# Eight places for the first weight tiles, modulation rows on GpSimd's queue, one conv group on TensorE, and block 1's top-k over two phases

## What is computed

```
mod = silu(c) @ w_ada + b_ada            # 1024 -> 6 x 1024: sh1 sc1 gt1 sh2 sc2 gt2
h1  = rmsnorm(x, g1) * (1 + sc1) + sh1
proj = h1 @ w_in + b_in                  # 512 pool, 512 conv value, 512 conv gate columns
pool_out = (box means of 2, 4, 8, 16 rows - hp) @ w_pool * pool_scale
conv_out = silu(layernorm(causal depthwise conv, 31 taps, of cv * sigmoid(cg)))
x  = x + gt1 * (concat(pool_out, conv_out) @ w_out + b_out)
h2 = rmsnorm(x, g2) * (1 + sc2) + sh2
q  = h2 @ w_query                        # 8 heads x 2 halves x 128
s  = q . sub_keys                        # 128 scores a half
top 16 of each half, top 16 of their 256 sums, softmax -> gate; 16384 experts
act = gelu(u_table[eid] . h2) * gate     # 128 rows of 4 KB for each token
x  = x + gt2 * sum(act * v_table[eid]);  y = rmsnorm(x, g_final)
```

## Time and profile before

| | |
|---|---|
| median of 3 runs | 3471.78 us (3471.12 to 3472.04) |
| profiled execution, time | 3469.63 us |
| profiled execution, span | 3467.7 us |
| mean granted TensorE clock | 0.82 |
| DMA | 1253.56 MB, mean 361 GB/s |
| VectorE, GpSimd, TensorE busy | 2125.2, 2283.7, 2206.3 us |

### The profile page before, as it was taken

One profiled execution on the slowest core, in us unless ns is written; L12 is line 12 of the kernel. 1 busy time (PEld: TensorE's weight loads), 2 busy tenths in 40 slices (PEclk: granted clock), 3 DMA queues, 4 the chain that ended last, 5 costly groups with the idle time before them and its releaser, 6 DMA issues.

```text
span 3467.7 us, 30586 instructions
## 1 busy us (share of the span) xinstructions
PE 2206.3 (64%) x9781; PEld 976.0 (28%) x9781; DVE 2125.2 (61%) x4835; ACT 360.6 (10%) x778; POOL 2283.7 (66%) x2213
## 2 busy tenths in 40 slices
PE   7873895467847899656448777454445444454576
PEld 6563452135512355211114444111111111111111
DVE  2345888645686677675655666667766776776301
ACT  3101141000111022100000010000000000000000
POOL 0012545676777777777757777777777777777675
PEclk9996897689978999888768999767777777776799
DMA  7666756899999999999989999999999999999998
GB/s 238 187 234 212 274 194 242 324 403 405 407 385 403 407 398 406 361 402 398 370 289 404 407 408 408 390 409 406 402 393 406 401 406 394 403 407 374 382 392 330
DMA packets 377968, 1253.56 MB, mean 361 GB/s; under 512 B 38056, under 2 KB 46912, under 8 KB 377793
## 3 DMA queue, kind: packets, MB, share of 16 engines
q0 software_dynamic: 304128, 1107.43, 82.3%
q1 hardware_dynamic: 51505, 100.14, 8.6%
q10 hardware_dynamic: 22176, 44.04, 3.4%
HBM read 1230.01 MB, written 22.06 MB: 361 GB/s over the span
## 4 chain that ended last, share of the span: by engine, by line
POOL 29%; DMA 27%; PE 24%; issue 10%; DVE 5%; SPq 3%; ACT 1%; DVEq 1%; POOLq 0%; ACTq 0%
DMA v_ring<-in_v_table_dram,eidt 21%; POOL u_ring L772 14%; POOL v_ring L789 13%; PE bank L1687 11%; PE bank L1526 4%; PE bank L1509 3%; SPq L535 2%; PE bank L1605 2%; DMA u_ring<-in_u_table_dram,eid 2%; DVE u_ring L1324 2%; DMA u_ring<-in_v_table_dram,eidt 1%; POOL u_ring L789 1%; DMA wring<-in_w_ada_dram 1%; PE bank L1581 1%; PE bank L1466 0%
## 5 line engine op out<-in xcount | busy, mean ns | idle before, releaser
L1687 PE MATMUL bank<-v_ring,act_x 128*32 128x512 f32 x3984 | 1184.2, 809 | 960.5 <-DMA v_ring<-in_v_table_dram,eidt 950.8
L1324 DVE CUSTOM_DVE_ANT_0 u_ring<-u_ring,h 128x1024 f32<-128x1024 f32 x1056 | 1281.8, 1226 | 785.4 <-DMA u_ring<-in_u_table_dram,eid 715.1
L772 POOL DMA_INDIRECT u_ring<-in_u_table_dram,eid x1024 | 1149.7, 1123 | 728.6 <-issue 299.8
L789 POOL DMA_INDIRECT v_ring<-in_v_table_dram,eidt x996 | 1036.0, 1040 | 396.4 <-issue 239.5
L1687 PEld LDWEIGHTS bank<-v_ring,act_x 128*32 128x32 f32 x3984 | 271.0, 135 | 1797.2 <-issue 1781.8
L1605 PE MATMUL bank<-hbuf,wring 128*128 128x128 f32 (+1 forms) x2048 | 243.8, 279 | 3.4 <-DMA wring<-in_w_query_dram 3.4
L1605 PEld LDWEIGHTS bank<-hbuf,wring 128*128 128x128 f32 x2048 | 236.4, 194 | 32.1 <-issue 28.4
L1526 PE MATMUL bank<-zc,dring 128*128 128x384 f32 (+1 forms) x512 | 194.4, 507 | 9.3 <-ACT dring L819 9.3
L1509 PE MATMUL bank<-hbuf,wring 128*128 128x384 f32 (+2 forms) x512 | 165.8, 483 | 23.4 <-ACT hbuf L832 22.5
L1509 PEld LDWEIGHTS bank<-hbuf,wring 128*128 128x128 f32 x512 | 99.0, 196 | 91.6 <-issue 64.0
L1581 PE MATMUL bank<-wring,mixt 128*128 128x512 f32 (+1 forms) x256 | 121.9, 627 | 0.0
(11 more groups left out here) (217 smaller groups left out, 1613.5 us busy)
## 6 DMA issues: line engine op xcount, KB each, us to landing
u_ring<-in_u_table_dram,eid POOLq DMA_INDIRECT x1024, 7.4
wring<-in_w_out_dram ACTq DMA_DIRECT2D x16, 1024.0 KB, 11.9
wring<-in_w_query_dram ACTq DMA_DIRECT2D x16, 1024.0 KB, 12.2
v_ring<-in_v_table_dram,eidt POOLq DMA_INDIRECT x996, 7.7
wring<-in_w_ada_dram SPq DMA_DIRECT2D x12, 1024.0 KB, 10.5
v_ring<-in_w_ada_dram SPq DMA_DIRECT2D x12, 1024.0 KB, 6.7
wring<-in_w_in_dram ACTq DMA_DIRECT2D x10, 1024.0 KB, 11.6
xr<-in_x_prompt_dram SPq DMA_DIRECT2D x16, 512.0 KB, 7.7
```

Source lines behind the costliest of these rows:

```text
L772: pool.indirect_dma_start(u_ring[:, n % NU], None, u_table[0], bass.IndirectOffsetOnAxis(ap=col, axis=0)).then_inc(u_in[n % NU], 16)
L789: pool.indirect_dma_start(place, None, v_table[0], bass.IndirectOffsetOnAxis(ap=eidt[:, b % RING, t:t + 1], axis=0)).then_inc(landed, 16)
L1324: dve.tensor_tensor_reduce(u_ring[:, n % NU], u_ring[:, n % NU], h2[:, b % 2], 1.0, 0.0, ALU.mult, ALU.add, dot[:, b % 2, k:k + 1]).then_i ...
L1687: last = pe.matmul(acc[h][j * S:(j + 1) * S, :], act_x[:, i % 2, j, a:a + S], v_place(n)[0][:, h * HALF:(h + 1) * HALF], start=(c == 0), s ...
```

## The change

1. The first eight weight tiles (modulations 0 to 3) have a place each: the four of before, three in `u_ring` and one in `v_ring`. After them the four places are used in turn as before. SP loads the keys, which lie in the eighth place, once modulation 3 has been computed.
2. GpSimd's queue instead of SP's: the load of `bout` for group 0, the stores of modulations 4 to 9, and the rows of `gt1` and of `mod2`'s first two rows. A row still waits for both stores of its pair. The samples' rows stay on SP and get semaphores of their own.
3. `PE_CONV` is 1: TensorE convolves one channel group of group 0, VectorE three. Behind it TensorE turns half of the keys and does the modulations 4 to 9 in a row, then the pool products; VectorE takes the modulations after all taps and the boxes.
4. In the layout group 1 starts at slot 5 (before: 2), and with it all steps of group 2 come 3 slots later. The exp and normalisation of block 0's part 0 stand in slot 5 (0). The top-k of block 0's parts 1 to 3 goes over slots 0 to 17 (0 to 12), and that of block b over 30 slots from 18 + 30(b - 1); block 1's four parts then begin at slots 18, 25, 33 and 40 and end at 46 (13, 18, 22, 27; 31).

```diff
-PLACE = [i % 4 if i < FIRST else (i - FIRST) % 2 for i in range(len(TILES))]
+PLACE = [i if i < 8 else i % 4 if i < FIRST else (i - FIRST) % 2 for i in range(len(TILES))]
...
-    at = 2
+    at = 5
...
-    first = [("exp", 0, 0), ("nrm", 0, 0)] + top_steps([(part, 0) for part in range(1, PARTS)] + [(part, 1) for part in range(PARTS)])
-    spread(first, 0, NCH)
-    for b in range(2, NB):
-        spread(top_steps([(part, b) for part in range(PARTS)]), (b - 1) * NCH + 8, b * NCH + 5)
-    spread(top_steps([(part, SB) for part in range(PARTS)]), LAST * NCH + 6, NB * NCH - 3)
+    spread(top_steps([(part, 0) for part in range(1, PARTS)]), 0, 18)
+    slots[5] += [("exp", 0, 0), ("nrm", 0, 0)]
+    for b in range(1, NB):
+        spread(top_steps([(part, b) for part in range(PARTS)]), 18 + 30 * (b - 1), 18 + 30 * b)
+    spread(top_steps([(part, SB) for part in range(PARTS)]), 18 + 30 * LAST, NB * NCH - 3)
...
+        more += [r[:, a:a + 2, :].rearrange("p a (b n) -> p (a b) n", n=HALF) for r, a in ((u_ring, 0), (u_ring, 2), (u_ring, 4), (v_ring, 4))]
...
-        PE_CONV = 2
+        PE_CONV = 1
...
+            pool.wait_ge(proj_ps, projected_at(0, 2, G - 1))
+            pool.dma_start(bout, b_out).then_inc(bout0_in, 16)
+            for n in range(4, 10):
+                pool.wait_ge(mod_taken, n + 1)
+                pool.dma_start(mod_dram[n], modst[:, n % 2]).then_inc(mod_stored[n % 2], 16)
+                if n % 2:
+                    for i in range(2):
+                        pool.wait_ge(mod_stored[i], 16 * (n // 2 - 1))
+                    out, ready = {5: (gt1[:, :], gt1_in), 7: (mod2[:, S2], mod2_in), 9: (mod2[:, A2], mod2_in)}[n]
+                    mod_row(pool, out, n // 2, 0, P, ready)
...
             taps(PE_CONV, G)
-            modulation(4)
-            modulation(5)
             boxes(0)
-            modulation(6)
-            modulation(7)
             dve.wait_ge(g2_in, 16 * 4)
-            modulation(8)
-            modulation(9)
+            for n in range(4, 10):
+                modulation(n)
...
-            convolve(0, 0, 0, NQ)
-            modulation(4)
-            modulation(5)
-            convolve(0, 1, 0, NQ)
-            modulation(6)
-            modulation(7)
+            for c in range(PE_CONV):
+                convolve(0, c, 0, NQ)
+            keys_turned(0)
+            keys_turned(1)
+            for n in range(4, 10):
+                modulation(n)
             for c in range(G):
                 pool_out(0, c)
-            modulation(8)
-            modulation(9)
-            keys_turned(0)
-            keys_turned(1)
```

More of the change, by code:

```diff
@@ L349, in build @@
             sem(n) for n in ("c_in", "par_in", "wp_in", "key_in", "bada_in", "g2_in", "gfin_in"))
-        w_at = [sem(f"w_at{i}") for i in range(4)]
+        w_at = [sem(f"w_at{i}") for i in range(8)]
         xr_in = [sem(f"xr_in{i}") for i in range(2)]
-        bout_in, gt1_in, mod2_in, gt2_in, h2_in, y_in = (
-            sem(n) for n in ("bout_in", "gt1_in", "mod2_in", "gt2_in", "h2_in", "y_in"))
+        bout0_in, gt1_in, mod2_in = (sem(n) for n in ("bout0_in", "gt1_in", "mod2_in"))
+        bout_in, gt1s_in, mod2s_in, gt2_in, h2_in, y_in = (
+            sem(n) for n in ("bout_in", "gt1s_in", "mod2s_in", "gt2_in", "h2_in", "y_in"))
         u_in = [sem(f"u_in{i}") for i in range(NU)]
@@ L356, in build @@
         mod_stored = [sem(f"mod_stored{i}") for i in range(2)]
+        mod_last = sem("mod_last")
         x1_stored = [sem(f"x1_stored{i}") for i in range(2)]
@@ L509, in v_place, with mod_row @@
             return u_ring[:, k - NV], u_in[k - NV], U_ALL // NU + m
+        def mod_row(eng, out, n, r, count, ready):
+            src = mod_dram[2 * n:2 * n + 2].rearrange("n (j q) c -> q n j c", q=S)[r]
+            eng.dma_start(out.rearrange("p (n j c) -> p n j c", n=2, j=4), src.unsqueeze(0).broadcast_to([count, 2, 4, P])).then_inc(ready, 16)
         def xr_at(*use):
@@ L526, in tile @@
                 sp.dma_start(places[PLACE[i]], tile_source(i)).then_inc(w_at[PLACE[i]], 16)
-            def mod_store(n):
-                sp.wait_ge(mod_taken, n + 1)
-                sp.dma_start(mod_dram[n], modst[:, n % 2]).then_inc(mod_stored[n % 2], 16)
-            def mod_row(out, n, r, count, ready):
-                src = mod_dram[2 * n:2 * n + 2].rearrange("n (j q) c -> q n j c", q=S)[r]
-                sp.dma_start(out.rearrange("p (n j c) -> p n j c", n=2, j=4), src.unsqueeze(0).broadcast_to([count, 2, 4, P])).then_inc(ready, 16)
-            def mod_wait(n):
-                for i in range(2):
-                    sp.wait_ge(mod_stored[i], 16 * (n - 1))
             def xr_load(i):
@@ L656, in _ @@
                 was = TILES[i - 4]
-                if was[0] == "ada" and was[1] >= 4 and was[2]:
-                    mod_store(was[1])
                 if was[0] == "q" and was[3]:
@@ L681, in _ @@
                     xr_load(3)
+                elif i == TILE_NO["q", 0, 0, 1]:
+                    sp.dma_start(gfin[:, :], g_final.rearrange("(a d) -> a d", a=1).broadcast_to([P, D])).then_inc(gfin_in, 16)
                 elif i == TILE_NO["q", 0, 2, 1]:
+                    for n in (10, 11):
+                        sp.wait_ge(mod_taken, n + 1)
+                        sp.dma_start(mod_dram[n], modst[:, n % 2]).then_inc(mod_last, 16)
                     x1_store(0)
@@ L685, in _ @@
             spill(PARTS - 1, 1)
-            mod_wait(5)
-            mod_row(mod2[:, GT2], 5, 0, P, gt2_in)
+            sp.wait_ge(mod_last, 16 * 2)
+            mod_row(sp, mod2[:, GT2], 5, 0, P, gt2_in)
             xr_load(4)
@@ L969, in _ @@
             ahead = [(c, q) for c in range(PE_CONV) for q in range(NQ)]
-            for c, q in ahead[:2]:
-                diagonals(0, c, q)
             act.wait_ge(modt_ready, 1)
@@ L974, in _ @@
                 x_columns(b)
+            for c, q in ahead[:2]:
+                diagonals(0, c, q)
             made = 2
@@ L982, in _ @@
                 if m == 0:
-                    while batch_freed(0, *ahead[made]) == 0:
+                    while made < len(ahead) and batch_freed(0, *ahead[made]) == 0:
                         diagonals(0, *ahead[made])
@@ L1199, in add_x @@
                 dve.wait_ge(mix_ps, b + 1)
-                dve.wait_ge(gt1_in, 16 if b < NB else 16 * (1 + NS))
+                if b < NB:
+                    dve.wait_ge(gt1_in, 16)
+                else:
+                    dve.wait_ge(gt1s_in, 16 * NS)
                 xr_wait(dve, "x1", b)
@@ L1215, in norm @@
                     dve.tensor_tensor_reduce(scratch[:, :], x, x, 1.0, 0.0, ALU.mult, ALU.add, nst[:, b % 2, 0:1]).then_inc(ss_done, 1)
-                dve.wait_ge(mod2_in, 16 * (2 if b < NB else 2 + 4 * NS * 2))
+                if b < NB:
+                    dve.wait_ge(mod2_in, 16 * 2)
+                else:
+                    dve.wait_ge(mod2s_in, 16 * 4 * NS * 2)
                 if 2 <= b < NB:
@@ L1572, in mix @@
                 if first and b == GROUPS[g][0]:
-                    pe.wait_ge(bout_in, 16 * (g + 1))
+                    if g:
+                        pe.wait_ge(bout_in, 16 * g)
+                    else:
+                        pe.wait_ge(bout0_in, 16)
                     pe.wait_ge(cm_ready, g + 1)
```

18 lines of the change are left out of this document (4 added, 14 removed).

## The result

| | before | changed |
|---|---|---|
| median of 4 runs, us | 3471.45 | 3430.94 (3429.68 to 3432.31) |
| ratio, 95% interval | | 0.9885 (0.9868 to 0.9902) |
| profiled execution, time; span | 3469.63; 3467.7 | 3431.25; 3429.4 |
| first dot of phases 0, 1, 2, 3 | 237.9, 628.1, 1023.4, 1382.9 | 237.7, 570.6, 967.4, 1338.5 |
| first dot of phases 4, 5, 6, 7 | 1800.1, 2163.5, 2506.1, 2846.7 | 1754.0, 2118.1, 2466.1, 2809.6 |

Faster by 40.5 us; 57 were forecast, and 3430.94 lies in the range. The windows of the changed kernel, cut at the first dots, stand against the earlier trace rows. Columns: the window, its length, busy time of PE, PEld, DVE, ACT and POOL with the number of instructions, TensorE's clock, DMA share, GB/s.

The account below looks back on a forecast made before the run. Later phases were taken as bound by DMA bytes, phase 0 by VectorE, then TensorE's chain. Terms -2 - 72 + 4 + 13 = -57 gave 3412.6 us profiled, 3415 median; range 3388 to 3446, own range 3400 to 3428.

Parts of the forecast that it names:

- Prologue, -2: Ahead of the first dot: conv costs 5 us, but the wait for the second modulation's last row goes; net gain 2.
- rival 2: Prologue: rows on GpSimd's queue come late, losing 21 us instead of winning 2; 3438 us; chance 0.12.
- Phase 0, -72: Phase 0: 318 us instead of 390, with TensorE late next and VectorE waiting twice for it.
- Step (1): Phase 0: VectorE's wait of 33 us for ScalarE's exp of block 0's part 0 goes.
- Step (2): Phase 0: two parts of block 1's top-k less, 38.4 us.
- Phase 1, +4: Phase 1: 46 us of added VectorE work is hidden in idle; three stores, 1.5 MB, cost 4 us.
- Rival 3: Phase 1: VectorE becomes the bound and gives the two parts back, 38 us; 3453 us; chance 0.12.
- near 551: Sign for the forecast: the dots of phase 1 start near 551 us.
- Phases 3 and 4, +13: SP's burst of 64 small transfers comes three slots later: one chunk fewer done meanwhile, 11 us, and 2 for weights.
- Later phases, nothing: Later phases: four top-k parts in 30 slots instead of 29 cost nothing.
- Rival 1: Phase 0: TensorE does not hold it, VectorE's 297 us plus 3 does; 18 us more gain, 3397; chance 0.14.
- rival 4: Prologue: three rows on GpSimd's queue take 45 us each, delaying norm and first gather; 3475 us and above; chance 0.03.

Follow-up runs that it names:

- the kernel with the three edits: Changed kernel with blocks 2 and 3's x read ahead of weight tile 42, the 1.6 MB behind put off, sample rows as 16 transfers and 3 copies: 3400.89 us.
- the last experiment: The kernel with the three edits, but with the groups' steps starting in slot 2 instead of 5: 3420.91 us, ratio 0.9853.
- the second profile: The changed kernel run and profiled once more, nothing changed: 3433.20 us, ratio 0.9887.
- the kernel with 16 transfers: Changed kernel with the sample's modulation rows as 16 small transfers and 3 copies in place of 64 small transfers: 3560.21 us, ratio 0.978.

## Why the prediction was right, and where not

*Prologue, -2.* Measured -0.2, by other sums. VectorE's taps and boxes had ended by 118.6, not 122, and modulations 6 and 7 ran from 119 to 124; but the tiles behind them came late, modulation 9 ended at 143.7 instead of 141, and the mixing began at 161.4 instead of 158. The rows on GpSimd's queue hid, as taken: 0.9 us to issue one, where I had 8 to 9. Their stores were the slow part, 3.0, 12.9 and 13.4 us from the issue's end to the landing, near the 11.3 of the earlier trace rows. The Trainium skill ("DMA: Bandwidth & Descriptors", "Anatomy of one DMA — SWDGE (gpsimd) path") would have 2.2 us for 64 KB. That holds for no store here; these were in flight beside 1 MB weight tiles, and the page's fixed-plus-bytes sum has no term for that. Nor did their own queue bring them past the tiles, as the argument against rival 2 had it. It did not matter: the last row was issued at 158.7, and block 0's norm at 186.4 waited for no row. The transposes were forecast at 194 and came at 197.6. What the sum did not have is TensorE's clock: the wait taken away had cost time twice, once as a stand and once as slower matmuls behind it. With it, the first gather was issued 2.2 us earlier than before (229.6 for 231.8), the forecast gain by luck. Its row then landed 8.1 us after the issue for 6.1. The runs agree: 8.1 in the kernel with the old layout and the new prologue, 6.1 in the one with the new layout and the old prologue; what holds the row back was not tested. And I took taps and modulations for small costs, where by the run with two conv groups on TensorE the conv group alone is a term of some 15 us, with as much against it.

*Phase 0, -72.* Measured -57.3: the failed step is its list of what is late next. It named TensorE only. The mechanism for that was right (two waits, 9.95 and 12.68 us; the 9.95 is just under the 10 to 25 forecast), but block 2's x, which SyncE reads behind a wait that ends at 280, was in no term. It put off the start of TensorE's chain: the projection began 106.7 us after the first dot (344.35) for the 90 forecast, and 93.6 after it (334.98) in the kernel with the three edits. With the x and what lies behind it out of the way the phase took 320.5 and 316.4 us, for the 318 forecast. Step (1) stood on more than the exp: moving that alone gave 5.6 us by the two profiles, on two chips, and no difference in the total. It took the start at slot 5 (36.8 us in the last experiment) and the x's place to be worth its 33. Step (2) was 38.4 us for two parts; undone, it cost 31.7.

*Phase 1, +4.* Measured +1.5 (396.8 us, at 400 GB/s), and +5.6 in the second profile: the size can't be told from nothing. Rival 3 asked for 420. The "near 551" for its first dot does not follow from the prediction's own 236 and 318, which make 554.

*Phases 3 and 4, +13.* Measured -1.0. One stall ahead of chunk 128's dots, and none for the sample's x, as forecast; but it took 24.3 us and not 35 to 40. The burst lasted 81.1 us for 89.2, and from its start to the stall's end were 88.4 us where the sum had 98: the term was mis-sized by these 10. One chunk fewer was done in that stretch, as forecast (20 dots, 24 before). That leaves some 3 of the 13, of which nothing was measured; so small a rest can't be placed. The burst as the cause is shown by the kernel with 16 transfers.

*Later phases, nothing.* This failed as well: +11.6 in phase 2, +8.3 in phases 5 and 6. The later start of the groups explains 4 of the first and, in phase 5, the whole 5.5 (going back to slot 2 gave 7.9 there). In phase 2 it brings a norm into chunk 64, where the finish of block 0 and a key search already are: 20.6 us, for 14.4 before and 13.7 with slot 2. For the rest, 7 to 8 in phase 2 and 3 in phase 6, the new order of the top-k is the candidate left; no run shows that by itself.

Rival 1 would have had waits for TensorE under 5 us, rival 2 a first dot beyond 245, rival 4 rows of 45 us: none came. In the profiled executions the gain is 38.4 us, for 57 forecast (the medians have 2 more): 15 less in phase 0, 19 less in phase 2 and behind phase 4, and 2 in the prologue, against 14 more in phases 3 and 4 and 2.5 in phase 1. That the total came within two thirds of the forecast is in part luck: two errors of 15 and 19 us were made smaller by one of 14 the other way.

## What to carry to other kernels

Where a long wait is removed from an in-order engine, look for every other input that this engine meets next, and when each is issued: here a load behind a weight's wait had been hidden by the very stall removed, and took back all but some 6 of 33 us when that stall alone was taken away. Follow the queue in the same way: taking one load from behind a burst only exposes the next one, while fewer transfers for the same rows removed the stall. A wait taken from TensorE can pay twice, since its clock may be lower behind a stand. And a sum of zero for a part with several edits may be two large terms; the one that was undone alone cost 15 us.
